# Order of the differential attention's stages: four frame stages first, the sample's four groups last

## What is computed

```python
def diff_attention(q, k, v, mask, lam, subln_g, lam_init):
    s = jnp.einsum('...qhcd,...khcd->...hcqk', q, k).astype(jnp.float32) * ATTN_SCALE
    s = jnp.where(mask, s, -jnp.inf)
    p = jax.nn.softmax(s, axis=-1)
    w = p[..., 0, :, :] - lam * p[..., 1, :, :]
    o = jnp.einsum('...hqk,...khe->...qhe', w.astype(v.dtype), v)
    return rms_norm(o, subln_g) * (1.0 - lam_init)

d_p = diff_prompt(qd, kd_all, vd_all, lam, subln_g[l], lam_init)    # blocks of 128 frames
kds = jnp.concatenate([cache_diff_k[l], kd_s], axis=1)
vds = jnp.concatenate([cache_diff_v[l], vd_s], axis=1)
d_s = diff_attention(qd_s, kds, vds, mask_s_diff, lam, subln_g[l], lam_init)
```

## Time and profile before

| what | us |
|---|---|
| three timed runs | 2769.49, 2767.01, 8953.95 (median 2769.49) |
| the profiled execution | 2765.84 |
| its span, first to last instruction | 2764.0 |
| TensorE busy in the span | 2640.0 |
| from the first differential load to the first exponentials of frame stage 0 | 604.62 to 636.69 |
| from there to the last exponentials of frame stage 3 | 636.69 to 1091.57 |
| to the first load of the output phase | 1102.72 |

### The profile page before, as it was taken

How to read it: one execution, slowest core, us unless ns; L and a number is a source line. 1 busy time by engine, 2 the same in 40 slices (tenths; PEclk the granted TensorE clock), 3 DMA queues, 4 the chain that set the end, 5 groups by cost and what they waited for, 6 DMA issues and landing times.

```text
span 2764.0 us, 48120 instructions
## 1 busy us (share of the span) xinstructions
PE 2640.0 (96%) x19852; PEld 1645.9 (60%) x19852; DVE 1581.0 (57%) x3263; ACT 1136.4 (41%) x2090; POOL 444.8 (16%) x530
## 2 busy tenths in 40 slices
PE   3999999978899998999999999999999999999998
PEld 1666666656667766555656565656565555656564
DVE  8777776768888773665462525353444444353516
ACT  4566666657889997544211111111120111111113
POOL 1211111105667666000000000000000000000001
PEclk9999999988999999999999999999999999999999
DMA  4123211142210000521101101010101010101003
GB/s 184 54 74 109 93 57 65 46 107 51 40 32 9 9 9 17 190 92 61 54 8 46 31 16 31 16 39 9 39 8 46 1 47 1 46 1 47 1 8 126
DMA packets 119197, 132.95 MB, mean 48 GB/s; under 512 B 42642, under 2 KB 97346, under 8 KB 117954
## 3 DMA queue, kind: packets, MB, share of 16 engines
q1 hardware_dynamic: 118978, 129.87, 14.8%
HBM read 92.20 MB, written 34.84 MB: 46 GB/s over the span
## 4 chain that ended last, share of the span: by engine, by line
PE 58%; DVE 1%; DMA 1%; ACT 0%; issue 0%; POOL 0%; POOLq 0%; ACTq 0%
PE y_ps L2325 6%; PE y_ps L2327 6%; PE y_ps L2326 6%; PE hnT_ps L2312 6%; PE hnT_ps L2313 6%; PE hnT_ps L2314 6%; PE mixT_ps L2312 6%; PE mixT_ps L2313 6%; PE mixT_ps L2314 6%; PE y_ps L2297 2%; PE y_ps L2299 2%; PE y_ps L2298 2%; DMA tail_buffers<-mix_scratch 1%; PE mixT_ps L2274 1%; PE hnT_ps L2284 0%; DVE tail_buffers L2054 0%
## 5 line engine op out<-in xcount | busy, mean ns | idle before, releaser
L2079 DVE SCALAR_TENSOR_TENSOR residual_rows<-y_ps,pair_scales,residual_rows 128x512 f32<-128x512 f32 (+1 forms) x374 | 276.8, 747 | 101.4 <-PE y_ps L2327 100.5
L2312 PE MATMUL hnT_ps<-ffn_inT_hi,tail_buffers 128*128 128x352 f16 x1056 | 330.0, 313 | 0.7 <-ACT ffn_inT_hi L2184 0.7
L2312 PE MATMUL mixT_ps<-ffn_inT_hi,tail_buffers 128*128 128x352 f16 x1056 | 330.1, 313 | 0.0
L2313 PE MATMUL hnT_ps<-ffn_inT_lo,tail_buffers 128*128 128x352 f16 x1056 | 330.0, 313 | 0.0
L2313 PE MATMUL mixT_ps<-ffn_inT_lo,tail_buffers 128*128 128x352 f16 x1056 | 330.0, 313 | 0.0
L2314 PE MATMUL hnT_ps<-ffn_inT_hi,tail_buffers 128*128 128x352 f16 x1056 | 330.0, 313 | 0.0
L2314 PE MATMUL mixT_ps<-ffn_inT_hi,tail_buffers 128*128 128x352 f16 x1056 | 330.0, 313 | 0.0
L2213 ACT ACTIVATE w_out_halves<-mixT_ps,pair_scales 128x352 f32<-128x352 f32 x66 | 36.6, 554 | 706.2 <-PE mixT_ps L2314 706.2
L1094 PE MATMUL z_ps<-w_in_hi_lo,normT_hi 128*128 128x384 f16 x816 | 268.5, 329 | 21.8 <-DVE w_in_hi_lo L681 21.8
L2067 DVE SCALAR_TENSOR_TENSOR w_out_halves<-hnT_ps,pair_scales,w_out_halves 128x352 f32<-128x352 f32 x66 | 38.5, 584 | 432.6 <-ACT w_out_halves L2213 432.6
L2325 PE MATMUL y_ps<-w_out_halves 128*128 128x512 f16 (+1 forms) x748 | 283.8, 379 | 0.0
(11 more groups left out here) (317 smaller groups left out, 5385.0 us busy)
## 6 DMA issues: line engine op xcount, KB each, us to landing
tail_buffers<-in_w_gate SPq DMA_DIRECT2D x11, 1024.0 KB, 5.4
tail_buffers<-in_w_up SPq DMA_DIRECT2D x11, 1024.0 KB, 8.0
tail_buffers<-in_w_down SPq DMA_DIRECT2D x22, 512.0 KB, 3.2
keys_values<-in_w_in SPq DMA_DIRECT2D x8, 1152.0 KB, 16.0
x_tile<-in_x SPq DMA_DIRECT2D x17, 512.0 KB, 3.7
tail_buffers<-mix_scratch SPq DMA_DIRECT2D x17, 512.0 KB, 3.7
residual_rows<-in_x SPq DMA_DIRECT2D x17, 512.0 KB, 4.6
out_y_prompt<-tail_buffers SPq DMA_DIRECT2D x16, 512.0 KB, 2.6
```

The source lines that it names most:

```text
L2079: nc.vector.scalar_tensor_tensor(out, YP[(2 * t + n) % 4][0:rows, :], PS[0:rows, i, F_YI:F_YI + 1], out, ALU.mult, ALU.add).then_inc(h_ok, 1)
L2312: nc.tensor.matmul(out, FH[w][:, k, c], nh, start=k == 0, stop=False)
L2313: nc.tensor.matmul(out, FH[w][:, k, c], nl, start=False, stop=False)
```

## The change

The frame stages 0 to 3 come first and the sample's groups last, so the stages begin at units 0, 32, 96, 192 and 320. What was loaded for the sample in the drain of phase_project is now loaded for frame stage 0 (load_first: four query tiles in eight loads, the first 512 keys of K2). The sample's cached keys are loaded at the start of phase_differential and its queries like those of any later stage; its values are still loaded in the drain. The waits on the cached keys, on K2 and on the cached values move to the sample's stage. LAST moves to the other query buffer, so the wait for its store now stands before that buffer's first load. The planner's code is otherwise the same and places the pieces by the new order.

```diff
--- before.py
+++ after.py
@@ -233,7 +233,7 @@
         CT = K1[:, :, CT_AT * P:(CT_AT + 2) * P].bitcast(f32)
         WB = [CT, K1[:, :, (CT_AT + 2) * P:(CT_AT + 4) * P].bitcast(f32)]
         K1C, K2D, Q1D, QLDF = diff_views(WHL)
-        at = (3 + NKT + 8) * HC * P + HC * (HD + 2)
+        at = (3 + NKT + 8) * HC * P + 4 * HC * (HD + 2)
         LAST = WHL[:, at:at + 2 * HS * HD].bitcast(f32)
         rows_out = lambda j: AO[:, :] if j < NT else LAST
         CR = AO[:, 0:2 * KVS * HD]
@@ -368,17 +368,20 @@
                     for n, V in enumerate((VH, VL)):
                         sp.dma_start(g.xv[n], V[:, xv[0]]).then_inc(x_stored, 16)
 
-                def load_sample_q():
-                    sp.dma_start(Q1D[0][:, :, 0:P], g.q1[rows(0), :].rearrange("p (h n) -> p h n", n=P)).then_inc(g.q_in[0], 16)
-                    sp.dma_start(QLDF[0][:, 0, :, 0:HD], g.ql[rows(0), :].rearrange("p (h d) -> p h d", d=HD)).then_inc(g.ql_in[0], 16)
-
-                def load_sample():
+                def load_first_q():
+                    for q in range(4):
+                        r = slice(q * P, (q + 1) * P)
+                        sp.dma_start(Q1D[0][:, :, q * P:(q + 1) * P], g.q1[r, :].rearrange("p (h n) -> p h n", n=P)).then_inc(g.q_in[0], 16)
+                    for q in range(4):
+                        r = slice(q * P, (q + 1) * P)
+                        sp.dma_start(QLDF[0][:, q, :, 0:HD], g.ql[r, :].rearrange("p (h d) -> p h d", d=HD)).then_inc(g.ql_in[0], 16)
+
+                def load_first():
                     sp.wait_ge(z_ok, 6 * NTT)
                     sp.wait_ge(x_stored, 48)
-                    sp.dma_start(K1C, g.xk.rearrange("p (h n) -> p h n", h=HC)).then_inc(g.kc_in, 16)
-                    load_sample_q()
-                    sp.dma_start(K2D[0:HD, :, NTT * P:NKT * P], g.xk.rearrange("p (h n) -> p h n", h=HC)[0:HD, :, :]).then_inc(g.k2_in[0], 16)
+                    load_first_q()
                     sp.wait_ge(kt_out, NT)
+                    sp.dma_start(K2D[0:HD, :, 0:4 * P], K1[0:HD, :, 0:4 * P]).then_inc(g.k2_in[0], 16)
                     sp.dma_start(K2D[0:HD, :, NT * P:NTT * P], K1[0:HD, :, NT * P:NTT * P]).then_inc(g.k2_in[0], 16)
                     sp.dma_start(K2D[HD:HD + 2, :, :].rearrange("p h n -> p (h n)").rearrange("p (m n) -> p m n", n=P),
                                  CM[:, :].unsqueeze(1).broadcast_to([2, HC * NKT, P])).then_inc(g.k2_in[0], 16)
@@ -429,7 +432,7 @@
                     if j > 1:
                         store_out(j - 2, 0)
                     if j == NTT:
-                        load_sample()
+                        load_first()
                     if j == NTT + 1:
                         load_sample_values_lo()
                     if 0 < j < NTT + 1:
@@ -1305,7 +1308,7 @@
 
 
     def __init__(self):
-        order = [NT // 4] + list(range(NT // 4))
+        order = list(range(NT // 4)) + [NT // 4]
         self.groups = [Group(4 * s + h, s, n, h) for s, n in enumerate(order) for h in range(HDIF)]
         self.units, self.first, self.last = [], [], {}
         users = {}
@@ -1470,14 +1473,17 @@
                         sp.dma_start(QL[stage % 2][:, q, :, 0:HD], g.ql[r:r + P, :].rearrange("p (h d) -> p h d", d=HD))\
                             .then_inc(ql_in[stage % 2], 16)
 
-                load_q1(1)
-                load_ql(1)
-                sp.dma_start(K2[0:HD, :, 0:4 * P], K1[0:HD, :, 0:4 * P]).then_inc(k2_in[1], 16)
                 sp.wait_ge(vm_zero, 1)
                 meta_v = slice(TS * HDIF * VW, (TS + 1) * HDIF * VW)
                 for r, V in ((0, VH), (2 * META, VL), (4 * META, VH)):
                     sp.dma_start(VM[r:r + META, :], V[DEC:DEC + META, meta_v]).then_inc(vm_in, 16)
-                sp.dma_start(K2[0:HD, :, 4 * P:NT * P], K1[0:HD, :, 4 * P:NT * P]).then_inc(k2_in[2], 16)
+                load_q1(1)
+                sp.dma_start(K2[0:HD, :, 4 * P:NT * P], K1[0:HD, :, 4 * P:NT * P]).then_inc(k2_in[1], 16)
+                for kv in range(KVS):
+                    sp.wait_ge(g.ao_stored[kv], 16 * NTT)
+                load_ql(1)
+                sp.dma_start(K1C, g.xk.rearrange("p (h n) -> p h n", h=HC)).then_inc(g.kc_in, 16)
+                sp.dma_start(K2[0:HD, :, NTT * P:NKT * P], g.xk.rearrange("p (h n) -> p h n", h=HC)[0:HD, :, :]).then_inc(k2_in[2], 16)
 
                 def store(gr):
                     sp.wait_ge(f_ok, gr.index + 1)
@@ -1491,9 +1497,6 @@
                             sp.wait_ge(s_ok, plan.stage_first[stage + 1])
                             load_q1(stage + 2)
                             sp.wait_ge(t2_ok, 4 * stage + 4)
-                            if stage == 0:
-                                for kv in range(KVS):
-                                    sp.wait_ge(g.ao_stored[kv], 16 * NTT)
                             load_ql(stage + 2)
                         store(groups[4 * stage + h])
                 for x in range(2):
@@ -1727,8 +1730,8 @@
                         pe.wait_ge(q2_out, gr.index + 1)
                     if u.k in plan.stage_first:
                         stage = plan.stage_first.index(u.k)
-                        if stage < 3:
-                            pe.wait_ge(k2_in[stage], (48, 16, 16)[stage])
+                        if stage < 2 or stage == n_stages - 1:
+                            pe.wait_ge(k2_in[min(stage, 2)], (48, 16, 16)[min(stage, 2)])
                     hc = 2 * gr.h + u.c
                     if u.kind == "meta":
                         pe.wait_ge(km_ok, 2)
@@ -1747,7 +1750,7 @@
                 def values(u):
                     pe.wait_ge(pool_lo_ok if plan.by_pool[u.k] else pl_ok, plan.lo_count[u.k])
                     gr = u.g
-                    if u.k == 0:
+                    if u.k == plan.stage_first[n_stages - 1]:
                         pe.wait_ge(g.v_in, 32)
                     first = u.k == plan.first[gr.index] or u.k - 1 == plan.last[gr.index, 0]
                     if first and gr.index:
@@ -1773,7 +1776,6 @@
                     last.then_inc(av_ok, 1)
 
                 pe.wait_ge(q_in[0], q_loads(0))
-                pe.wait_ge(g.kc_in, 16)
                 for p in plan.pieces[0]:
                     max_piece(p)
                 q2T(groups[0])
@@ -1786,6 +1788,8 @@
                     for p in plan.at[k] if k < K else ():
                         if p.g.stage > seen:
                             seen = p.g.stage
+                            if not p.g.frame:
+                                pe.wait_ge(g.kc_in, 16)
                             pe.wait_ge(q_in[seen % 2], q_loads(seen))
                         max_piece(p)
                     nxt = plan.starts(k + 4)
```

## The result

The kernel after takes **2777.01 us** (median of seven runs), the kernel before, timed beside it, 2767.57: a ratio of 1.0038, with a 95% interval of 1.0029 to 1.0048. That is 8 to 13 us more, where +3.3 was forecast; the time lies in the range, and within 2%.

What follows compares the result with a forecast made beforehand. Head bound by slow clock and short steps, stage 0 by VectorE, last stage by TensorE, tail by small operations. Terms +0.5 -23.0 +2.9 +2 +0.6 +21.5 -1.2 = +3.3 on 2765.84: 2769 us, range 2758 to 2784.

Steps and rivals of the forecast that it cites:

- Part 3: Frame stage 0: bound by VectorE; more max pieces cost +2.9 and a clock fall at its start +2.
- Four more pieces cost 4 x 0.73 = +2.9: Frame stage 0: 37 max pieces instead of 33 on VectorE, which bounds it; 0 to +4.
- The clock's term of +2 at the start: Start of stage 0: clock falls in the head, returns in about 4 us, half of that lost; 0 to +13.
- Part 1: Drain of the projection phase: more loads on SP delay it 3 to 5 us, about using up 4.0 slack; +0.5.
- Part 2: New head: stage 0's first exponential comes near 613.7 instead of 636.69; -23.0.
- Part 5: Sample groups at the end: 32 units at 0.54 us, plus query copies, stalls and hand-over; +21.5 (17.3 to 28.15).
- the end goes cold: Slower rival, sample at the end: thin units let the clock fall, costing 28.15 us; +6.6, 2776; chance 0.17.
- Parts 4 and 6: Stages 1 to 3 keep their lengths but some sample pieces show, +0.6; tail from last exponential to output phase, -1.2.
- Stage 0 stays cold: Slower rival, stage 0: 26 us at half the clock instead of 4; +11, 2780; chance 0.12.
- The sample hides: Faster rival: sample at ScalarE's rate (17.3), pieces in idle VectorE time, no clock fall; 2760; chance 0.18.
- nothing moves: Rival for the whole kernel: work changes place at equal cost, 2766; inside the forecast's own range, no separate chance.

Runs made afterwards that it cites:

- e5: Kernel after, with the second of two max pieces at the unit beside the next group's query transposes put one unit later: 2771.28 us (1.0017).
- e4: Kernel after, with the low parts of stage 0's 256-column units made by GpSimd instead of VectorE: 2774.09 us (1.0028).
- e3: Kernel after, with 152 keep-busy products instead of 64 and added identity products in the head's TensorE gaps: 2776.47 us (1.0032).
- e7: Kernel after, with K2's meta copy and first pieces earlier at the head, output-scale operations earlier and 48 keep-busy products instead of 96 at the tail: 2772.49 us.
- e9: Kernel after, with four identity products added on TensorE behind the values of each of the sample's 32 units: 2777.01 us (1.0031).
- e8: Kernel after, with the edits of e1, e5 and e7 together: 2766.77 us (0.9998).
- e1: Kernel after, with the sample's value loads moved from the drain to the start of phase_differential, the query-store wait behind the last window store: 2776.15 us (1.0032).

## Why the prediction was wrong

The direction and the large terms were right; the sum was +3.3 where the trace has +8.5.

- **Part 3, stage 0: the failed step.** "Four more pieces cost 4 x 0.73 = +2.9" counts VectorE's work. The total came near (+4.9; +6.2) for a wrong reason. e5 keeps all pieces in the stage (38 by the planner's list; I had 37) and takes 52.64 us, so the extra pieces cost nothing that shows. What cost 5.4 us is where two of them stand: beside the transposes, in whose bank the wait begins. At the turn into stage 1 the wait alone is the smaller part of it, 1.5 of 4.4 by e4; the rest is the clock that fell behind it. I had counted how many pieces fall into the stage, not laid them beside the transposes and the ratio. The clock's term of +2 at the start was too large: by e3 0.6, though the clock was low for 8 us, not 4. And the dip of the earlier trace rows, which I read as one with TensorE busy without a break, began near 672.5 in a gap of 1.48 us (the piece at 673.35 ends it): a sign of such waits that I passed over.
- **Part 1, the drain: mis-sized.** +0.5, measured +2.9. I took all of the 4.0 us between SP's last issue and the next phase as slack. The phase begins 1.5 to 1.6 us after the last engine is through, so the slack was 604.80 - 1.58 - 600.62 = 2.6. SP was through 5.5 us later, measured from the window store: 5.5 - 2.6 = 2.9. I had the delay (3 to 5) nearly right and the slack wrong.
- **Part 2, the head.** -23.0, measured -21.8. Missed: ScalarE's copy of K2's meta keys, which the sample's units did not need and the frame's first unit does (0.7 by e7), and the low clock (0.9 by e3).
- **Part 5, the sample at the end.** +21.5, measured +22.2. The clock fell to 0.50 within the second group; by e9 that cost 1.0 us, not the 6.6 of the rival "the end goes cold". The rival's condition came true and its price did not. The rule of the Trainium skill beside it (TensorE: Matmul & The Clock Gate, "HAM oscillation — how this bites in real kernels") speaks of bursts of matmuls shorter than the waits between them. The trace does not show that case: in the 2 us in which the clock fell TensorE was busy for 1.32, with no gap over 0.62.
- **Parts 4 and 6.** Stages 1 to 3 +0.1 (+0.6), tail -1.1 (-1.2). Both right, the tail by its chain too: the last reciprocal came 4.05 us after the last exponential (forecast 4.0). By the planner's list 20 pieces of later stages are done at the end of stage 0, not 19.
- **The rivals.** "Stage 0 stays cold" has nearly the right place, and the dips are there, but the stage is not cold from its start: they come at the two turns, mostly behind the wait at the bank, and in e5 stage 0 is short without a warm head. "The sample hides" and "nothing moves" fell.

What stays open: whether either order gains from e4's edit once the bank is free, and what brings or spares a dip of the clock, at the turns and in stage 1. The order itself is worth at most a few us: with its side effects mended and its tail shortened it is level with the kernel before (e8), and 3 to 4 us faster with e4's edit added.

## To carry to other kernels

When a change moves work among queues, lay the new list out instruction by instruction around each shared buffer: which use holds the bank that the next one takes, and what stands before its release. A sum of busy times does not see a bank that frees 2.7 us late, nor the clock that may fall behind it. And slack is counted to the last engine's end, less what the start of a phase itself takes, not to the start of the phase.

## What the hardware showed

- After 2.66 us without a product on TensorE in the kernel after (667.64 to 670.30), in a stretch that had run at 1.00, the granted clock was 0.50 until about 676, though TensorE was busy again. Over all profiles the two turns of stage 0 have 13 waits of 2.65 to 2.69 us; the clock fell to 0.50 at 12 of them and stayed at 1.00 at one (e4). At the 15 turns with one piece, whose longest gap is 1.34 to 1.48 us, it fell at six. With the same gap of 1.39 us it fell in e8 and stayed in e5, so the length of the gap alone did not decide.
- Half the clock made a stretch hardly longer: in the sample TensorE was busy for 20.49 of 22 us at a mean clock of 0.67, and with the clock at 1.00 and 119 more products in those 22 us the 32 units took only 1.0 us less.
- The differential phase began 1.3 to 1.7 us after the last engine had finished the phase before, whichever engine it was: TensorE (1.47 in before, 1.32 in e3) or SP (1.58 in after, 1.65 in e1). The output phase is no such case: in the kernel before it began 2.36 us after SP's last issue (1100.36 to 1102.72), behind which SP waits for its stores to land.
